# The end of an MoE block: dividing eight expert rows per token between VectorE and TensorE, and moving a gate to GpSimd

## The chip, the cores and the metric

The kernel runs on one core of one Trainium2 chip. The metric is device time in microseconds (us) of one execution, on-chip from start to finish. A core has TensorE (PE, matrix products into PSUM), VectorE (DVE), ScalarE (ACT), GpSimd (POOL) and SyncE (SP), which here only issues DMA transfers. The engines run their own instruction streams and meet at semaphores.

## What is computed

Two transformer layers (feed-forward, attention, per-layer gates) and then a third block that ends in a mixture of experts, all in float32, for 512 tokens of width 1024. The change touches only what comes after the last expert. In the reference:

```
out = jnp.zeros((T + 1, D), jnp.float32).at[rows].add(ys * wts[:, None])   # routed_experts: top 8 of 64 experts
return (routed + shared).reshape(B, S, D).astype(h.dtype)                  # moe_ffn
x = x + g2 * moe_ffn(h, ...)                                               # second_block
return rmsnorm_2(x, final_g)
```

So for each token: shared-expert row, plus eight weighted expert rows, times the gate g2, plus the residual x, and an RMS norm of the sum.

## The kernel before

The kernel is written out by hand per engine. Each engine's order is the order of the Python code, and each semaphore wait is explicit. Up to about 3293 us of 3352 it is bound by TensorE, which runs every product as three (high and low parts). The change begins behind that.

**Layout.** The 512 tokens are four tiles t = 0..3 of 128 tokens (one per partition) by 1024 values. Each expert block's outputs are scattered by GpSimd's indirect DMA to a DRAM tensor `slot_rows`[t, token, slot k, 1024], where slot k = 0..7 is the token's k-th expert in order of expert number. At the end the 32 pieces (t, k), 512 KB each, are fetched back by SyncE in the order of its code, into 16 buffers `rows[0..15]` in `big` and `h_buf`: first the 16 "early" ones, k = 0..3, then 16 "late" ones in the order of the table `LATE`. Late fetch number i waits until buffer i has been read.

**Adding.** `sh_tok[t]` (in `xn_buf`) holds the shared expert's row. VectorE adds slots 0, 1, 3 and 4 into it, one `scalar_tensor_tensor` per tile and slot (`add_row`). TensorE adds slots 2, 5, 6 and 7 in PSUM, as products with a diagonal matrix of the slot's weights (`sum_rows`; `eye_w`, made by ScalarE); one tile and slot is 2 products of 512 columns, which the chip runs as 4 MATMUL instructions. Between its first four pieces and the rest stand 44 small products (`keep_clock`) that do no work.

**Finishing.** `gated_early` (VectorE, two instructions per tile): y = sh_tok * g2, then y + x. `add_late`: the PSUM sum * g2 into `x_tok` (in `mixed_buf`), then y + that. ScalarE squares and sums y and takes the root (`fin["std"]`). `final_norm`: reciprocal, then y * inverse * gain in two halves of 512. SyncE sends each finished tile out. All four early gates stand ahead of the first `add_late`; from there VectorE alternates `add_late(t)` and `final_norm(t - 1)`. GpSimd has nothing to do after its last scatter.

**Semaphores.** `fin["row"]` counts VectorE's adds, `fin["part"]` TensorE's early ones, `fin["mm"]` finished tiles in PSUM, `fin["sum"]` finished sums; `row_in`, `row_last` count landings (16 each); `o_out[s]` tells that a scatter has landed.

Of the kernel before, what the change touches and what calls it, by code (L numbers as in the profile page):

```python
# [129 lines left out]
def block_kernel(nc, dr, out, stop_at=None):  # L130
    with ExitStack() as ctx:
# [320 lines left out]
        fin = {n: sem(f"fin_{n}") for n in ("row", "part", "mm", "sum", "std", "y")}  # L452
# [21 lines left out]
        LATE = [(t, 4) for t in range(TT)] + [(t, k) for t in range(TT) for k in range(5, TOP_K)]  # L474
        PE_ROWS = [2, 5, 6, 7]
# [109 lines left out]
        def _(sp):  # L585
# [59 lines left out]
            for st in STAGES:  # L645
# [50 lines left out]
                elif st == "moe":  # L696
# [73 lines left out]
                    for i, (t, k) in enumerate(LATE):  # L770
                        if i == 0:
                            for s in range(2):
                                after(o_out[s], more * 16 + 16)
# [4 lines left out]
                        if 8 <= i < 12:
                            sp.wait_ge(fin["part"], i - 7)
                        else:  # L780
                            sp.wait_ge(fin["row"], (i if i < 8 else i - 4) + 1)
                        fetch(rows[i], t, k, row_last[t] if k == 4 else row_in[t])
# [816 lines left out]
        def _(act):  # L1599
# [277 lines left out]
            for st in STAGES:  # L1877
# [75 lines left out]
                elif st == "moe":  # L1953
# [112 lines left out]
                    for t in range(TT):  # L2066
                        act.wait_ge(fin["sum"], t + 1)
                        link(nc.scalar.activation(sil_buf[:, :], sh_tok[:, t, :], ACT.Square, accum_out=ssq[:, t:t + 1]))
                        nc.scalar.activation(sdev[:, t:t + 1], ssq[:, t:t + 1], ACT.Sqrt, bias=eps[:, 0:1], scale=1.0 / D
                                             ).then_inc(fin["std"], 1)  # L2070

        @block.gpsimd
        def _(pool):
# [47 lines left out]
            for st in STAGES:  # L2122
# [16 lines left out]
                else:  # L2139
# [64 lines left out]

        @block.vector
        def _(dve):
# [680 lines left out]
            def add_row(n):  # L2888
                k, t = (0, 1, 3, 4)[n // TT], n % TT
                if k == 4:  # L2890
                    dve.wait_ge(row_last[t], 16)
                elif t == 0:
                    dve.wait_ge(row_in[k], 64)
                if n >= TT:
                    dve.wait_ge(fin["row"], n - TT + 1)
                w = slot_w[:, t * TOP_K + k:t * TOP_K + k + 1]
                nc.vector.scalar_tensor_tensor(out=sh_tok[:, t, :], in0=late_row[t, k] if k == 4 else rows[k * TT + t], scalar=w,
                                               in1=sh_tok[:, t, :], op0=ALU.mult, op1=ALU.add).then_inc(fin["row"], 1)

            def combine():  # L2900
                for n in range(EARLY * TT):
                    add_row(n)

                def gated_early(t):
                    y = sh_tok[:, t, :]
                    dve.wait_ge(fin["row"], 3 * TT + t + 1)
                    link(nc.vector.tensor_tensor(y, y, g2_row, ALU.mult))
                    link(nc.vector.tensor_tensor(y, y, x_tok[:, t, :], ALU.add))

                def add_late(t):  # L2910
                    y = sh_tok[:, t, :]
                    dve.wait_ge(fin["mm"], t + 1)
                    link(nc.vector.tensor_tensor(x_tok[:, t, :], ps_t[:, 2 * t * T:2 * t * T + D], g2_row, ALU.mult))
                    nc.vector.tensor_tensor(y, y, x_tok[:, t, :], ALU.add).then_inc(fin["sum"], 1)
# [288 lines left out]
```

## Time and profile before

| what | us |
|---|---|
| median of 3 runs (lowest, highest) | 3352.76 (3351.64, 3355.06) |
| profiled execution, whole | 3353.4 |
| its span, first to last instruction | 3351.6 |
| PE / DVE / ACT / POOL busy | 3266.6 / 1933.7 / 1720.9 / 1341.5 |
| DMA rate in the last four of 40 slices | 389, 372, 367, 300 GB/s |

The table shows a kernel whose TensorE is 97% busy over the whole span. That says nothing of the last 50 us, which have other limits and are read from the timeline of that stretch. In the views, L12 is line 12 of the kernel; "x8" after a row is a run of eight merged instructions; square brackets give the idle time of the engine before the row and what ended it.

### The profile page before, as it was taken

What the parts mean: (1) busy time and instruction counts of PE and PEld (TensorE: products, weight loads), DVE (VectorE), ACT (ScalarE), POOL (GpSimd) and SP (SyncE); (2) the same over time, 40 slices, a digit from 0 to 9 for tenths busy, and PEclk for the clock granted to TensorE, in tenths of its full rate; (3) what the DMA queues carried; (4) which work ended last, traced back from release to release, by engine and by line L of the source; (5) the groups of instructions that cost most, each with busy time, mean ns of one, the idle gap of its engine ahead of it and who ended that gap; (6) DMA issues with size and microseconds to landing.
All of it is one profiled execution on the core that took longest, in us unless ns stands there. A gap on an engine that the chain in (4) does not pass through costs nothing.

```text
span 3351.6 us, 48653 instructions
## 1 busy us (share of the span) xinstructions
PE 3266.6 (97%) x16528; PEld 2637.9 (79%) x16528; DVE 1933.7 (58%) x2446; ACT 1720.9 (51%) x2086; POOL 1341.5 (40%) x675
## 2 busy tenths in 40 slices
PE   8999999999999999999999999999899999999997
PEld 7888887778888788888778888788776788888785
DVE  4335684653354433551473333456676799999898
ACT  5552334555523555321545542512452788888884
POOL 3444442044444444444134444344212344444441
PEclk9999999999999999999999999999999999999999
DMA  3224331022244222443322233223102899999997
GB/s 126 99 95 162 126 104 51 15 93 94 100 155 136 86 95 99 144 144 113 126 76 94 100 94 94 94 88 111 39 20 107 332 377 385 384 391 389 372 367 300
DMA packets 128100, 534.42 MB, mean 159 GB/s; under 512 B 24464, under 2 KB 24720, under 8 KB 100112
## 3 DMA queue, kind: packets, MB, share of 16 engines
q1 hardware_dynamic: 107136, 499.63, 41.8%
q0 software_dynamic: 20736, 33.60, 2.7%
q8 instruction: 52, 0.85, 0.1%
q14 instruction: 32, 0.26, 0.0%
q10 hardware_dynamic: 144, 0.08, 0.0%
HBM read 531.64 MB, written 41.94 MB: 171 GB/s over the span
## 4 chain that ended last, share of the span: by engine, by line
PE 55%; issue 27%; POOL 9%; DVE 4%; DMA 3%; ACT 1%; POOLq 0%; SPq 0%; DVEq 0%; ACTq 0%
PE ps L873 15%; PE ps L875 15%; PE ps L874 15%; POOL w_lo L2085 9%; DMA big<-in_exp_gu 2%; PE ps L1447 2%; PE ps L1045 1%; PE ps L1070 1%; PE ps L1055 1%; PE ps L893 1%; PE ps L1177 1%; PE ps L1215 1%; PE ps L1431 0%; DMA big<-slot_rows 0%; PE ps L1131 0%
## 5 line engine op out<-in xcount | busy, mean ns | idle before, releaser
L2085 POOL TENSOR_TENSOR w_lo<-stage_buf,w_hi 128x1024 fp32r<-128x1024 f32 (+1 forms) x396 | 970.4, 2451 | 1493.0 <-ACT w_hi L1611 1493.0
L1611 ACT ACTIVATE w_hi<-stage_buf 128x1024 fp32r<-128x1024 f32 (+1 forms) x396 | 413.9, 1045 | 1184.5 <-PE ps L875 1122.3
L873 PE MATMUL ps<-x_hi,w_hi 128*128 128x512 f32 x1984 | 774.3, 390 | 4.3 <-POOL w_lo L2085 2.8
L874 PE MATMUL ps<-x_lo,w_hi 128*128 128x512 f32 x1984 | 773.0, 390 | 0.0
L875 PE MATMUL ps<-x_hi,w_lo 128*128 128x512 f32 x1984 | 772.9, 390 | 0.0
L873 PE MATMUL ps<-hid,w_hi 128*128 128x512 f32 x1312 | 519.4, 396 | 2.8 <-issue 1.7
L875 PE MATMUL ps<-hid,w_lo 128*128 128x512 f32 x1312 | 512.2, 390 | 0.0
L874 PE MATMUL ps<-hid,w_hi 128*128 128x512 f32 x1312 | 511.5, 390 | 0.0
L873 PEld LDWEIGHTS ps<-x_hi,w_hi 128*128 128x128 f32 x1984 | 372.6, 188 | 85.2 <-POOL w_lo L2085 3.9
L875 PEld LDWEIGHTS ps<-x_hi,w_lo 128*128 128x128 f32 x1984 | 372.6, 188 | 77.2
L874 PEld LDWEIGHTS ps<-x_lo,w_hi 128*128 128x128 f32 x1984 | 372.7, 188 | 76.7
L2349 DVE TENSOR_TENSOR sq_buf<-ps,rstd 128x512 f32<-128x512 f32 x88 | 60.9, 692 | 406.2 <-PE ps L875 398.9
L873 PEld LDWEIGHTS ps<-hid,w_hi 128*128 128x128 f32 x1312 | 246.5, 188 | 55.0 <-issue 4.6
L875 PEld LDWEIGHTS ps<-hid,w_lo 128*128 128x128 f32 x1312 | 246.4, 188 | 52.7
L874 PEld LDWEIGHTS ps<-hid,w_hi 128*128 128x128 f32 x1312 | 246.9, 188 | 49.0 <-issue 0.2
L2354 DVE TENSOR_TENSOR hid<-tmp_buf,hid 128x512 f32 x88 | 164.3, 1867 | 82.6 <-ACT hid L1702 82.6
L2171 POOL DMA_INDIRECT slot_rows<-stage_buf,mask x72 | 184.6, 2563 | 24.8 <-issue 20.5
L2154 POOL CAST mask<-mask 128x2 int32 (+2 forms) x77 | 71.0, 922 | 308.0 <-PE ps L1447 242.1
L2844 DVE TENSOR_TENSOR hid<-s_buf,hid 128x2048 fp32r<-128x2048 f32 x71 | 162.7, 2292 | 16.1 <-ACT hid L1997 14.8
L2844 DVE TENSOR_TENSOR hid<-big,hid 128x2048 fp32r<-128x2048 f32 x72 | 161.7, 2285 | 9.4 <-ACT hid L1997 9.4
L2844 DVE TENSOR_TENSOR hid<-h_buf,hid 128x2048 fp32r<-128x2048 f32 x72 | 161.6, 2284 | 0.5 <-ACT hid L1997 0.5
L2220 DVE TENSOR_TENSOR acc<-acc,sq_buf 128x512 f32<-128x512 f32 x64 | 152.4, 2381 | 2.2
(401 smaller groups left out, 4858.3 us busy)
## 6 DMA issues: line engine op xcount, KB each, us to landing
stage_buf<-in_gu SPq DMA_DIRECT2D x176, 512.0 KB, 3.2
big<-in_exp_gu SPq DMA_DIRECT2D x72, 1024.0 KB
h_buf<-in_exp_gu SPq DMA_DIRECT2D x72, 1024.0 KB, 12.7
s_buf<-in_exp_dn SPq DMA_DIRECT2D x72, 1024.0 KB
stage_buf<-in_down SPq DMA_DIRECT2D x64, 512.0 KB, 3.6
stage_buf<-in_down SPq DMA_DIRECT2D x32, 384.0 KB, 3.2
sil_buf<-in_ada SPq DMA_DIRECT2D x24, 512.0 KB, 4.0
tmp_buf<-in_ada SPq DMA_DIRECT2D x24, 512.0 KB, 4.2
```

Source lines behind the costliest of these rows:

```text
L873: nc.tensor.matmul(o, a_hi, b_hi, start=start, stop=False)
L874: nc.tensor.matmul(o, a_hi, b_lo, start=False, stop=False)
L875: return nc.tensor.matmul(o, a_lo, b_hi, start=False, stop=stop)
L1447: last = nc.tensor.transpose(ps[:, k // 4, (k % 4) * P:(k % 4) * P + P], xg[s][:, k * P:k * P + P], eye[:, :])
L1611: nc.scalar.activation(w_hi[s][:, 0:n], stage[s][:, 0:n], ACT.Copy).then_inc(upper_done, 1)
L2085: nc.gpsimd.tensor_tensor(w_lo[s][:, 0:n], stage[s][:, 0:n], w_hi[s][:, 0:n].bitcast(F32), ALU.subtract).then_inc(parted, 1)
L2154: nc.gpsimd.tensor_copy(idx[:, s, c0:c1], table[:, b, c0:c1]).then_inc(bk["staged"], 1)
L2171: nc.gpsimd.indirect_dma_start(out=dr["slots"].rearrange("t p k n -> (t p k) n"), out_offset=bass.IndirectOffsetOnAxis(ap=idx[:, at, 1:2], ...
L2220: link(nc.vector.tensor_tensor(acc[:, :], acc[:, :], sq[:, 0, :], ALU.add))
L2349: nc.vector.tensor_tensor(sq[:, 1, :], ps[:, 1, :], rstd[:, :], ALU.mult).then_inc(evac_done, 1)
L2354: nc.vector.tensor_tensor(hid_buf[:, bass.ds(i * T + NF * T, T)], tmp[:, 0, :], hid_buf[:, bass.ds(i * T, T)].bitcast(F32), ALU.subtract). ...
L2844: nc.vector.tensor_tensor(raw_lo[j], raw[s][j], raw_hi[j].bitcast(F32), ALU.subtract).then_inc(raw_parted[j], 1)
```

## The change

- **Division of slots.** VectorE adds slots 0, 2, 4, 6; TensorE slots 1, 3, 5, 7. Each still adds 16 pieces.
- **Order of the late fetches.** `LATE` was (0..3, 4), then (0,5) (0,6) (0,7) (1,5) ... It is now (0,4) (0,6) (0,5) (0,7) (1,4) (1,6) (1,5) (1,7) (2,4) (2,6) (3,4) (3,6) (2,5) (2,7) (3,5) (3,7): pairs for VectorE and for TensorE in turn. The engines wait for a pair at a time; the last piece, (3,7), has a wait of its own. Fetch (3,4) waits in addition for VectorE's first late add, because its landing semaphore is used a second time.
- **Gate and residual** (y * g2, + x) move from VectorE to GpSimd, two instructions per tile, as soon as VectorE has added that tile's two late slots. The values are the same.
- **VectorE's order** is now: early adds, late pairs of tiles 0, 1, 2, `add_late(0)`, late pair of tile 3, `add_late(1)`, `final_norm(0)`, and so on; the last tile's `add_late` is done in halves of 512, and so are ScalarE's squares of it.
- **TensorE** has no `keep_clock` products any more.

```diff
-        PE_ROWS = [2, 5, 6, 7]
...
+        DVE_ROWS, PE_ROWS = [0, 2, 4, 6], [1, 3, 5, 7]
+        dve_landed = [(row_last[0], 32), (row_last[2], 32), (row_in[0], 96), (row_last[0], 64)]
+        pe_landed = [(row_last[1], 32), (row_last[3], 32), (row_in[1], 96), (row_in[3], 80)]
+        final_landed = (row_in[2], 80)
...
-                        if 8 <= i < 12:
-                            sp.wait_ge(fin["part"], i - 7)
-                        else:
-                            sp.wait_ge(fin["row"], (i if i < 8 else i - 4) + 1)
-                        fetch(rows[i], t, k, row_last[t] if k == 4 else row_in[t])
+                        slot, at = i // TT, i % TT
+                        sp.wait_ge(fin["part" if slot in PE_ROWS else "row"], slot // 2 * TT + at + 1)
+                        if (t, k) == (TT - 1, 4):
+                            sp.wait_ge(fin["row"], 2 * TT + 1)
+                        final = (t, k) == (TT - 1, TOP_K - 1)
+                        fetch(rows[i], t, k, (final_landed if final else pe_landed[t] if k in PE_ROWS else dve_landed[t])[0])
...
-                pe.wait_ge(row_in[2], 64)
-                for t in range(TT):
-                    add(t, 0, rows[2 * TT + t]).then_inc(fin["part"], 1)
-                keep_clock(0, 44, add=True)
-                for t in range(TT):
-                    pe.wait_ge(row_in[t], 64 + 48)
-                    for j in range(1, 4):
-                        last = add(t, j, late_row[t, PE_ROWS[j]])
-                    last.then_inc(fin["mm"], 1)
+                for j, k in enumerate(PE_ROWS[:2]):
+                    pe.wait_ge(row_in[k], 64)
+                    for t in range(TT):
+                        add(t, j, rows[k * TT + t]).then_inc(fin["part"], 1)
+                for t in range(TT - 1):
+                    pe.wait_ge(*pe_landed[t])
+                    add(t, 2, late_row[t, PE_ROWS[2]])
+                    add(t, 3, late_row[t, PE_ROWS[3]]).then_inc(fin["mm"], 1)
+                t = TT - 1
+                pe.wait_ge(*pe_landed[t])
+                add(t, 2, late_row[t, PE_ROWS[2]])
+                pe.wait_ge(*final_landed)
+                for c in range(2):
+                    add(t, 3, late_row[t, PE_ROWS[3]], (c,)).then_inc(fin["mm"], 1)
...
+                    t = TT - 1
+                    act.wait_ge(fin["sum"], TT)
+                    link(nc.scalar.activation(sil_buf[:, 0:T], sh_tok[:, t, 0:T], ACT.Square, accum_out=half_ssq))
+                    link(nc.scalar.activation(half_mean, half_ssq, ACT.Identity, bias=eps[:, 0:1], scale=1.0 / D))
+                    act.wait_ge(fin["sum"], TT + 1)
+                    link(nc.scalar.activation(sil_buf[:, T:D], sh_tok[:, t, T:D], ACT.Square, accum_out=ssq[:, t:t + 1]))
+                    nc.scalar.activation(sdev[:, t:t + 1], ssq[:, t:t + 1], ACT.Sqrt, bias=half_mean, scale=1.0 / D
+                                         ).then_inc(fin["std"], 1)
...
+                    for t in range(TT):
+                        y = sh_tok[:, t, :]
+                        pool.wait_ge(fin["row"], 2 * TT + 2 * t + 2)
+                        link(nc.gpsimd.tensor_tensor(y, y, g2_row, ALU.mult))
+                        nc.gpsimd.tensor_tensor(y, y, x_tok[:, t, :], ALU.add).then_inc(fin["gated"], 1)
...
+                def late_rows(t):
+                    dve.wait_ge(*dve_landed[t])
+                    for j, k in enumerate(DVE_ROWS[2:]):
+                        dve.wait_ge(fin["row"], 2 * TT + 2 * t + 1 if j else TT + t + 1)
+                        add_row(t, k, late_row[t, k])
+                def add_late(t, a=0, n=D):
+                    y, x = sh_tok[:, t, a:a + n], x_tok[:, t, a:a + n]
+                    dve.wait_ge(fin["gated"], t + 1)
+                    dve.wait_ge(fin["mm"], t + 1 + a // T)
+                    link(nc.vector.tensor_tensor(x, ps_t[:, 2 * t * T + a:2 * t * T + a + n], g2_row[:, a:a + n], ALU.mult))
+                    nc.vector.tensor_tensor(y, y, x, ALU.add).then_inc(fin["sum"], 1)
...
-                for t in range(TT):
-                    gated_early(t)
-                for t in range(TT):
-                    add_late(t)
-                    if t >= 1:
-                        final_norm(t - 1)
-                final_norm(TT - 1)
+                for t in range(3):
+                    late_rows(t)
+                add_late(0)
+                late_rows(3)
+                add_late(1)
+                final_norm(0)
+                add_late(2)
+                final_norm(1)
+                for c in range(2):
+                    add_late(3, c * T, T)
+                final_norm(2)
+                final_norm(3)
```

VectorE's stream behind the early adds. Names: `xn_buf` is sh_tok, `rot` holds g2, `mixed_buf` is x_tok, `ps` is PSUM; a row without "big" or "h_buf" is gate, residual or norm. Before:

```order
L2897 SCALAR_TENSOR_TENSOR xn_buf<-big,pt_buf,xn_buf 128x1024 [waits fin_row,row_in3]
L2897 SCALAR_TENSOR_TENSOR xn_buf<-big,pt_buf,xn_buf 128x1024 [waits fin_row] x3
L2897 SCALAR_TENSOR_TENSOR xn_buf<-big,pt_buf,xn_buf 128x1024 [waits fin_row,row_last0]
L2897 SCALAR_TENSOR_TENSOR xn_buf<-big,pt_buf,xn_buf 128x1024 [waits fin_row,row_last1]
L2897 SCALAR_TENSOR_TENSOR xn_buf<-big,pt_buf,xn_buf 128x1024 [waits fin_row,row_last2]
L2897 SCALAR_TENSOR_TENSOR xn_buf<-big,pt_buf,xn_buf 128x1024 [waits fin_row,row_last3]
L2907 TENSOR_TENSOR xn_buf<-xn_buf,rot 128x1024 [waits fin_row]
L2908 TENSOR_TENSOR xn_buf<-xn_buf,mixed_buf 128x1024 [waits dve_own]
L2907 TENSOR_TENSOR xn_buf<-xn_buf,rot 128x1024 [waits fin_row,dve_own]
L2908 TENSOR_TENSOR xn_buf<-xn_buf,mixed_buf 128x1024 [waits dve_own]
L2907 TENSOR_TENSOR xn_buf<-xn_buf,rot 128x1024 [waits fin_row,dve_own]
L2908 TENSOR_TENSOR xn_buf<-xn_buf,mixed_buf 128x1024 [waits dve_own]
L2907 TENSOR_TENSOR xn_buf<-xn_buf,rot 128x1024 [waits fin_row,dve_own]
L2908 TENSOR_TENSOR xn_buf<-xn_buf,mixed_buf 128x1024 [waits dve_own]
L2913 TENSOR_TENSOR mixed_buf<-ps,rot 128x1024 [waits fin_mm,dve_own]
L2914 TENSOR_TENSOR xn_buf<-xn_buf,mixed_buf 128x1024 [waits dve_own]
```

After (L2915 is `add_row`, L2936 and L2937 are `add_late`):

```order
L2915 SCALAR_TENSOR_TENSOR xn_buf<-big,pt_buf,xn_buf 128x1024 [waits fin_row] x3
L2915 SCALAR_TENSOR_TENSOR xn_buf<-big,pt_buf,xn_buf 128x1024 [waits fin_row,row_last0]
L2915 SCALAR_TENSOR_TENSOR xn_buf<-big,pt_buf,xn_buf 128x1024 [waits fin_row]
L2915 SCALAR_TENSOR_TENSOR xn_buf<-h_buf,pt_buf,xn_buf 128x1024 [waits fin_row,row_last2]
L2915 SCALAR_TENSOR_TENSOR xn_buf<-h_buf,pt_buf,xn_buf 128x1024 [waits fin_row]
L2915 SCALAR_TENSOR_TENSOR xn_buf<-big,pt_buf,xn_buf 128x1024 [waits fin_row,row_in0]
L2915 SCALAR_TENSOR_TENSOR xn_buf<-big,pt_buf,xn_buf 128x1024 [waits fin_row]
L2936 TENSOR_TENSOR mixed_buf<-ps,rot 128x1024 [waits fin_mm,fin_gated]
L2937 TENSOR_TENSOR xn_buf<-xn_buf,mixed_buf 128x1024 [waits dve_own]
L2915 SCALAR_TENSOR_TENSOR xn_buf<-big,pt_buf,xn_buf 128x1024 [waits fin_row,row_last0]
L2915 SCALAR_TENSOR_TENSOR xn_buf<-big,pt_buf,xn_buf 128x1024 [waits fin_row]
L2936 TENSOR_TENSOR mixed_buf<-ps,rot 128x1024 [waits fin_mm,fin_gated]
L2937 TENSOR_TENSOR xn_buf<-xn_buf,mixed_buf 128x1024 [waits dve_own]
```

The eight rows on `rot` and `mixed_buf` between the adds and the first `ps` row are gone, and each pair of late adds waits for one landing semaphore. `add_late` now also waits for GpSimd (`fin_gated`).

GpSimd's last rows, after its last scatter (L2190, the same instruction as L2171 before). Before, the stream ended with that scatter. After:

```order
L2174 REGISTER_ALU
L2190 DMA slot_rows<-stage_buf,mask 4096x1024 [waits bk_staged]
L2226 TENSOR_TENSOR xn_buf<-xn_buf,rot 128x1024 [waits fin_row]
L2227 TENSOR_TENSOR xn_buf<-xn_buf,mixed_buf 128x1024 [waits pool_own]
L2226 TENSOR_TENSOR xn_buf<-xn_buf,rot 128x1024 [waits fin_row]
L2227 TENSOR_TENSOR xn_buf<-xn_buf,mixed_buf 128x1024 [waits pool_own]
```

Eight instructions stand here now, two per tile (the first two tiles are shown); all read two operands in SBUF (`xn_buf` with `rot`, `xn_buf` with `mixed_buf`).

SyncE's late fetches, from the first on. Before:

```order
L753 DMA big<-slot_rows 128x1024 [waits o_out0,o_out1,fin_row]
L753 DMA big<-slot_rows 128x1024 [waits fin_row] x3
L753 DMA h_buf<-slot_rows 128x1024 [waits fin_row]
L756 REGISTER_ALU
L753 DMA h_buf<-slot_rows 128x1024 [waits o_out0,fin_row]
L753 DMA h_buf<-slot_rows 128x1024 [waits o_out1,fin_row]
L753 DMA h_buf<-slot_rows 128x1024 [waits fin_row]
L753 DMA big<-slot_rows 128x1024 [waits fin_part] x4
L753 DMA big<-slot_rows 128x1024 [waits fin_row] x4
```

After:

```order
L758 DMA big<-slot_rows 128x1024 [waits o_out0,o_out1,fin_row]
L761 REGISTER_ALU
L758 DMA big<-slot_rows 128x1024 [waits o_out0,fin_row]
L758 DMA big<-slot_rows 128x1024 [waits fin_row]
L758 DMA big<-slot_rows 128x1024 [waits o_out1,fin_row]
L758 DMA h_buf<-slot_rows 128x1024 [waits fin_part] x4
L758 DMA big<-slot_rows 128x1024 [waits fin_row] x4
L758 DMA big<-slot_rows 128x1024 [waits fin_part] x4
```

The waits for the last two scatters (`o_out0`, `o_out1`) moved from the sixth and seventh late fetch to the second and fourth. The four fetches into `h_buf` and the last four now wait for TensorE (`fin_part`).

## Rows read from the trace of the kernel before

**Rows 1.** Timeline, VectorE, last 50 us: start, length, instruction, count, idle before.
```profile
3312.49 9.66 DVE L2897 SCALAR_TENSOR_TENSOR xn_buf<-big,pt_buf,xn_buf 128x1024 f32<-128x1024 f32 x8 [4.98 <-DMA big<-slot_rows]
3322.07 1.22 DVE L2907 TENSOR_TENSOR xn_buf<-xn_buf,rot 128x1024 f32<-128x1024 f32 x1
...
3330.88 1.23 DVE L2908 TENSOR_TENSOR xn_buf<-xn_buf,mixed_buf 128x1024 f32<-128x1024 f32 x1
3332.14 1.22 DVE L2913 TENSOR_TENSOR mixed_buf<-ps,rot 128x1024 f32<-128x1024 f32 x1
...
3338.97 1.22 DVE L2913 TENSOR_TENSOR mixed_buf<-ps,rot 128x1024 f32<-128x1024 f32 x1
...
3342.89 1.22 DVE L2913 TENSOR_TENSOR mixed_buf<-ps,rot 128x1024 f32<-128x1024 f32 x1
...
3347.77 0.75 DVE L2921 SCALAR_TENSOR_TENSOR mixed_buf<-xn_buf,small,rstd 128x512 f32<-128x512 f32 x1
```
**Rows 2.** Groups by line, VectorE, 3312 to 3352 us: busy us, mean ns, idle before.
```profile
L2897 DVE SCALAR_TENSOR_TENSOR xn_buf<-big,pt_buf,xn_buf 128x1024 f32<-128x1024 f32 x8 | 9.7, 1280 | 5.0 <-DMA big<-slot_rows 5.0
...
L2907 DVE TENSOR_TENSOR xn_buf<-xn_buf,rot 128x1024 f32<-128x1024 f32 x4 | 4.9, 1224 | 0.1
L2913 DVE TENSOR_TENSOR mixed_buf<-ps,rot 128x1024 f32<-128x1024 f32 x4 | 4.9, 1219 | 0.0
```
**Rows 3.** Timeline, SyncE, 3293 to 3352 us.
```profile
3339.08 9.80 SPq L786 DMA_DIRECT2D out<-mixed_buf  x4
```
**Rows 4.** Source line of the fetches, windows of one: start, then us to landing.
```profile
L753 SPq DMA_DIRECT2D big<-slot_rows x1: 320/320/320, 3300.4 to 3300.4; - x1
...
DMA to landing us min/median/max: 14.7/14.7/14.7
...
L753 SPq DMA_DIRECT2D h_buf<-slot_rows x1: 320/320/320, 3308.0 to 3308.0; - x1
...
L753 SPq DMA_DIRECT2D h_buf<-slot_rows x1: 320/320/320, 3310.3 to 3310.3; - x1
...
L753 SPq DMA_DIRECT2D big<-slot_rows x1: 429/429/429, 3319.2 to 3319.2; - x1
...
DMA to landing us min/median/max: 13.9/13.9/13.9
```
**Rows 5.** Timeline, TensorE, 3300 to 3345 us.
```profile
3307.39 6.39 PE L1512 MATMUL ps<-big,tmp_buf 128*128 128x512 f32 x8 [6.35 <-DMA big<-slot_rows]
...
3321.85 7.03 PE L1512 MATMUL ps<-h_buf,tmp_buf 128*128 128x512 f32 x16
...
3332.15 10.46 PE L1512 MATMUL ps<-big,sq_buf 128*128 128x512 f32 x24
```
**Rows 6.** Windows: length, busy of PE, PEld, DVE, ACT, POOL, clock, DMA.
```profile
3302.00:3306.00 4.00, 0.00 (x0) 0.00 (x0) 4.00 (x4) 0.09 (x1) 1.56 (x2) 1.00 0.99 354
3306.00:3312.00 6.00, 4.61 (x6) 2.06 (x7) 1.51 (x2) 0.00 (x0) 0.00 (x0) 0.50 1.03 417
```
**Rows 7.** GpSimd's two-operand instructions: timeline at 2187 us, group, one source line.
```profile
2187.36 4.71 POOL L2085 TENSOR_TENSOR w_lo<-stage_buf,w_hi 128x1024 fp32r<-128x1024 f32 x2 [20.73 <-ACT w_hi L1611]
...
L2085 POOL TENSOR_TENSOR w_lo<-stage_buf,w_hi 128x1024 fp32r<-128x1024 f32 x364 | 906.8, 2492 | 1412.9 <-ACT w_hi L1611 1412.8
...
L2098 POOL TENSOR_TENSOR pt_buf<-pt_buf,sil_buf x2: 627/628/629, 2374.2 to 2375.5; 128x256 f32<-128x256 f32 x2
```
**Rows 8.** Timeline around 290 us, VectorE and GpSimd; last, durations (min/median/max) of L2220.
```profile
290.41 0.69 DVE L2219 TENSOR_TENSOR sq_buf<-h_buf 128x512 f32 x1
291.14 2.77 DVE L2220 TENSOR_TENSOR acc<-acc,sq_buf 128x512 f32<-128x512 f32 x1
...
290.58 2.78 POOL L2085 TENSOR_TENSOR w_lo<-stage_buf,w_hi 128x1024 fp32r<-128x1024 f32 x1 [1.69 <-ACT w_hi L1611]
...
L2220 DVE TENSOR_TENSOR acc<-acc,sq_buf x64: 691/2766/2866, 275.9 to 2533.9; 128x512 f32<-128x512 f32 x64
```
**Rows 9.** Timeline, VectorE, 2187.0 to 2192.5 us, beside the first row of 7.
```profile
2188.04 0.69 DVE L2394 TENSOR_SCALAR big<-ps 128x512 f32<-128x512 f32 x1 [1.12 <-PE ps L893]
```

More of the change, by code:

```diff
@@ L451, in block_kernel @@
         row_last = [sem(f"row_last{t}") for t in range(TT)]
-        fin = {n: sem(f"fin_{n}") for n in ("row", "part", "mm", "sum", "std", "y")}
+        fin = {n: sem(f"fin_{n}") for n in ("row", "part", "gated", "mm", "sum", "std", "y")}
         RAW = 2048
@@ L473, in block_kernel @@
         last_hi, last_lo = raw_hi[0], raw_lo[0]
-        LATE = [(t, 4) for t in range(TT)] + [(t, k) for t in range(TT) for k in range(5, TOP_K)]
-        PE_ROWS = [2, 5, 6, 7]
+        LATE = [(t, k) for t in range(2) for k in (4, 6, 5, 7)] + [(t, k) for t in (2, 3) for k in (4, 6)] + [
+            (t, k) for t in (2, 3) for k in (5, 7)]
+        DVE_ROWS, PE_ROWS = [0, 2, 4, 6], [1, 3, 5, 7]
+        dve_landed = [(row_last[0], 32), (row_last[2], 32), (row_in[0], 96), (row_last[0], 64)]
+        pe_landed = [(row_last[1], 32), (row_last[3], 32), (row_in[1], 96), (row_in[3], 80)]
+        final_landed = (row_in[2], 80)
         late_row = {tk: rows[i] for i, tk in enumerate(LATE)}
@@ L482, in block_kernel @@
         ssq, sdev, sinv = small[:, 64:68], small[:, 68:72], small[:, 72:76]
+        half_ssq, half_mean = small[:, 76:77], small[:, 77:78]
         before, iota_t = mask[:, 0:P], mask[:, P:P + T]
@@ L1508, in sum_rows, with add @@
             def sum_rows():
-                def add(t, j, row):
-                    for c in range(2):
+                def add(t, j, row, cs=(0, 1)):
+                    for c in cs:
                         done = nc.tensor.matmul(ps[:, 2 * t + c, :], eye_w[4 * t + j], row[:, c * T:(c + 1) * T],
@@ L2065, in _ @@
                     evacuate(1, more_n + 1)
-                    for t in range(TT):
+                    for t in range(TT - 1):
                         act.wait_ge(fin["sum"], t + 1)
@@ L2886, in routed @@
                 hidden_low(1, more_n + 1)
[L2888 to L2892, printed above, removed]
-                    dve.wait_ge(row_in[k], 64)
[L2894 to L2914, printed above, removed]
+            def add_row(t, k, row):
+                w = slot_w[:, t * TOP_K + k:t * TOP_K + k + 1]
+                nc.vector.scalar_tensor_tensor(out=sh_tok[:, t, :], in0=row, scalar=w, in1=sh_tok[:, t, :],
+                                               op0=ALU.mult, op1=ALU.add).then_inc(fin["row"], 1)
@@ new lines, in combine @@
+            def combine():
+                for j, k in enumerate(DVE_ROWS[:2]):
+                    dve.wait_ge(row_in[k], 64)
+                    for t in range(TT):
+                        if j:
+                            dve.wait_ge(fin["row"], t + 1)
+                        add_row(t, k, rows[k * TT + t])
+                def late_rows(t):
[9 more added lines that the diff above has]
+                    nc.vector.tensor_tensor(y, y, x, ALU.add).then_inc(fin["sum"], 1)
@@ L2923, in final_norm @@
                     ins.then_inc(fin["y"], 1)
-                for t in range(TT):
-                    gated_early(t)
-                for t in range(TT):
-                    add_late(t)
-                    if t >= 1:
-                        final_norm(t - 1)
-                final_norm(TT - 1)
+                for t in range(3):
[10 more added lines that the diff above has]
+                final_norm(3)
             for st in STAGES:
```

## The prediction

> **What bounds the kernel now.** I read the timeline of the last 50 us first, engine by engine, because the whole-span shares (TensorE 97%) describe what lies ahead of the change. VectorE's rows [rows 1] are the ones to see: from 3312.49, when the pieces it had waited 4.98 us for land, to 3348.52 (3347.77 + 0.75) it runs without a gap worth naming. In those 36.0 us stand 8 adds (9.66), 8 instructions of gate and residual (3322.07 to 3332.14, 10.1) and the late sums and norms (16.4). Every other engine only has to stay ahead of it. The groups by line [rows 2] give the prices: 1.28 us for an add as recorded, 1.22 for a 1024-wide two-operand instruction; back to back an add takes 9.66 / 8 = 1.21. SyncE's last rows [rows 3] are four output transfers, and the span ends 3.1 us behind VectorE's last instruction (3351.6 - 3348.5). Two things lie close behind: the landings of the fetches [rows 4], the last issued at 3319.2 and landed 13.9 later, at 3333.1; and TensorE, which works until 3342.6 (3332.15 + 10.46) [rows 5], 0.3 us before VectorE takes up its last tile at 3342.89 [rows 1].
>
> **The landings.** The late piece fetched at 3300.4 lands at 3315.1, the last at 3333.1: 14 pieces later in 18.0 us, 1.29 us each, with the transfer engines full (share 0.99 and 1.03) [rows 4, 6]. The change moves the same bytes, so I keep this raster of landings and only put other pieces on it. The new order needs its second late fetch at the moment a scatter has landed, which before was the fetch at 3308.0, and its fourth at 3310.3 [rows 4]. At 3308.0 the early slot 3 and (0,4) are still under way, to 3313.8, so the queue is not empty and (0,6) lands at 3315.1. From there (1,4) and (1,6) are down by 3320, (2,4) and (2,6) by 3325, (3,4) and (3,6) by 3327.6, the last by 3333.1. The extra wait of (3,4) for VectorE's first late add ends near 3316.3, with eight pieces (10 us) still queued: it costs nothing. The fetches behind TensorE's slot 3 can be issued from 3314 to 3320, also in time.
>
> **TensorE.** It starts on slot 1 near 3302.2 rather than on slot 2 at 3307.39, and drops the 44 idle products. A 512-wide instruction is 7.03 / 16 = 0.44 us at the full clock, 6.39 / 8 = 0.80 where the granted clock was 0.50 [rows 5, 6]; that low clock followed 5 us in which TensorE did nothing (1.00 still in 3302 to 3306) [rows 6]. A piece is 4 instructions, 1.8 us. Slot 1: to 3309.3; wait for slot 3's landing at 3312.5; slot 3: to 3319.6; tile 0: 3323.3; tile 1: 3326.9; tile 2 lands at 3330.2 and is done at 3333.8; the last tile is done at 3337.5. The idle spells are now 3.2 and 3.3 us, shorter than the one of 5 that lowered the clock. I cost the dropped products at nothing: VectorE, below, asks for tile 0 at 3331 and for the last at 3351. If that cover goes, half clock from the start is 64 x 0.80 = 51 us, to 3353.4.
>
> **VectorE's own work after the change.** By 3312.2 it has added slots 0 and 2 (slot 2 lands at 3307.4, where TensorE's wait for it ended [rows 5], and four adds take 4.8), so it stands where it stood before. Then: 8 late adds at 1.2, four of them behind their own predecessor (+0.07), 9.9; four late sums, three of 2.45 and the last in halves, 2.8, makes 10.1; four norms, 6.2, from the raster 3338.97 to 3342.89 = 3.92 for one sum and one norm [rows 1]. Sum 26.2. Removed: 10.1 of gate and residual. ScalarE's squares of the last half hide behind `final_norm(2)`, as before.
>
> **What the move to GpSimd costs.** The price of one instruction is in the trace: a GpSimd subtraction of two 1024-wide SBUF operands takes 4.71 / 2 = 2.36 us back to back, and a multiplication of 256 columns in place 0.63, the same rate [rows 7]. Eight of them are 18.8 us, which would fit beside VectorE if the two ran side by side. They don't. At 290.58 [rows 8] GpSimd starts while a VectorE instruction with SBUF operands runs until 291.10; it needs 2.78 instead of 2.36 and ends at 293.36, 2.26 behind VectorE's end. VectorE's next one, L2220, which also takes both operands from SBUF, starts at 291.14 and ends at 293.91, 0.55 behind GpSimd: 2.77 us for 0.69 of work. That is no accident of one place: the median of its 64 instances is 2.766, the least 0.691 [rows 8]. A VectorE instruction that reads PSUM, at 2188.04 in the middle of a GpSimd one, keeps its 0.69 [rows 7, 9]. So two-SBUF-operand instructions of the two engines exclude each other, whole instruction by whole instruction. All late adds, the second half of each late sum and both halves of each norm are of that kind; only the products with `ps` are not.
>
> The Trainium skill says the same of the cause (SBUF — State Buffer, "Who interferes with whom"): a VectorE instruction with two SBUF inputs and a GpSimd instruction that reads SBUF share a read port as an exclusive lock, and the later one is blocked fully. [...] The skill also warns (Perfetto Trace Analysis, "GPSIMD Engine Instruction") that GpSimd's recorded durations are unreliable and that spacing should be used; by the recorded mean of 2.49 instead of the spacing of 2.36, eight would be 1.0 us more.
>
> **The schedule.** At 3315.1 VectorE adds tile 0's pair, to 3317.5. GpSimd's first instruction (3317.6 to 3320.0) falls into VectorE's wait for tile 1 (2.4 us, free of charge). Then they alternate. VectorE stands behind GpSimd: 2.3 us before its second add of tile 1; 1.9 and 2.3 around tile 2's pair; 1.2 in `add_late(0)` (the `ps` product covers the rest); 2.3 before tile 3's pair; 1.2 in `add_late(1)`; 2.1 in `final_norm(0)`. Sum 13.3, from 3321 to 3345.4, when GpSimd is through. Each blocked one ends 0.14 sooner after its release than it takes alone (0.55 against 0.69 [rows 8]), seven times, -0.9. Landing waits are 2.4 and 0.5.
>
> 3315.1 + 26.2 + 13.3 - 0.9 + 2.9 = 3356.6, against 3348.5: +8.1 us. In terms: 10.1 saved; 13.3 - 0.9 lost to exclusion; 5.5 of waiting for landings where VectorE had work before (3312.5 to 3315.1, and 2.9); 0.6 for the halves and the pairs' own order; minus 0.4 that VectorE waited for the root of tile 0. The span becomes 3359.7 and the execution 3361.5, as the profiled one was 3353.4 for a span of 3351.6. That one lies 0.6 above the median of 3352.76, so the forecast is 3360.8.
>
> **Rivals.**
> - *Exclusion does not bite here (the other side: not slower).* If GpSimd's instructions ran freely, the schedule has no blocked time and waits 2.4 and 2.7 for landings: 3315.1 + 26.2 + 5.1 = 3346.4, -2.1: 3350.6. It decides from 5 us of blocked time downward. For it: the last 50 us themselves show no exclusion, since GpSimd computes nothing there. Against: the median of L2220's 64 instances. 0.08.
> - *VectorE wins the turns and GpSimd fills the gaps.* Then the bound is the sum of excluding work from 3315.1: GpSimd 8 x 2.26 = 18.1, VectorE 8 x 1.2 + 4 x 1.15 + 8 x 0.67 = 19.6, plus little of the last `ps` halves: 3353.5, +5.0: 3357.8. For it: GpSimd, too, is the one that waits in rows 8. Against: there it got the very next turn. 0.16.
> - *The fetches run dry.* SyncE issues in order; the two scatter waits now stand ahead of 14 fetches rather than 10. If a scatter lands 5 us later, VectorE's pairs shift by 3 to 5 us: 3364 to 3366. Against: the fetches still under way at 3308.0. 0.08.
> - *TensorE stays at the low clock* without its filler: 3353.4 for its end, then the last half sum, root and norm, 4.2: 3357.6, beyond the schedule by 1.0: 3361.8. 0.04.
>
> **How the numbers follow.** The schedule above has 0.64, its own range is 3358.5 to 3363.5. A measurement of this kernel can tell 0.2%, 6.7 us, from no change. Of the 0.64 I put 0.56 beyond that and 0.08 within; the freed-port rival gives 0.06 within and 0.02 faster; the second 0.15 within, 0.01 slower; the last two 0.12 slower. Faster 0.02, same 0.29, slower 0.69. The range 3355 to 3366 leaves out the first rival and little else.
>
> **What would show it.** Right: L2915's late adds, L2937 and L2944 with durations of 2 to 3.5 us where GpSimd's L2226 and L2227 run, L2936 at 1.2 throughout; GpSimd done near 3345; VectorE's last instruction near 3356.6; TensorE idle and no one waiting for it. Wrong: L2937 and the late adds at 1.2 with GpSimd's beside them (then the kernel is slightly faster); VectorE waiting for landings past 3326 (then the fetch order is the matter); VectorE waiting for `ps` (then the clock is).

## The result, and the profile after

The changed kernel is slower: 3362.66 us, median of 9 runs (3358.29 to 3369.93), against 3354.28 us (3351.15 to 3355.26) of before beside it. The ratio is 1.0026, 95% interval 1.0017 to 1.0034. The forecast was 3360.8. The profiled execution took 3360.6 us, its span (first to last instruction) is 3358.8.

Executions differ by several us before the changed part begins (VectorE's first slot-0 add started at 3297.87 before and 3297.51 after, and between 3293.69 and 3301.92 in the kernels below). So all traces are compared by the **tail**: from the start of that first add to the end of VectorE's last instruction. Before it is 50.65 us (3297.87, in the row below, to 3348.52 [rows 1]); after it is 58.2 (3297.51 to 3355.71), so +7.5. Behind VectorE's last instruction the span has 3.1 us more in both. The row of before, of VectorE's timeline:

```profile
3297.87 4.86 DVE L2897 SCALAR_TENSOR_TENSOR xn_buf<-big,pt_buf,xn_buf 128x1024 f32<-128x1024 f32 x4
```

VectorE's timeline after (start, length, instruction, count, idle before); it answers to [rows 1]:

```profile
3297.51 4.86 DVE L2915 SCALAR_TENSOR_TENSOR xn_buf<-big,pt_buf,xn_buf 128x1024 f32<-128x1024 f32 x4
3306.67 4.87 DVE L2915 SCALAR_TENSOR_TENSOR xn_buf<-big,pt_buf,xn_buf 128x1024 f32<-128x1024 f32 x4 [4.29 <-DMA big<-slot_rows]
3314.40 2.60 DVE L2915 SCALAR_TENSOR_TENSOR xn_buf<-big,pt_buf,xn_buf 128x1024 f32<-128x1024 f32 x2 [2.86 <-DMA big<-slot_rows]
3319.52 4.74 DVE L2915 SCALAR_TENSOR_TENSOR xn_buf<-h_buf,pt_buf,xn_buf 128x1024 f32<-128x1024 f32 x2 [2.52 <-DMA h_buf<-slot_rows]
3324.61 6.43 DVE L2915 SCALAR_TENSOR_TENSOR xn_buf<-big,pt_buf,xn_buf 128x1024 f32<-128x1024 f32 x2 [0.36 <-DMA big<-slot_rows]
3330.96 1.21 DVE L2936 TENSOR_TENSOR mixed_buf<-ps,rot 128x1024 f32<-128x1024 f32 x1
3332.21 2.34 DVE L2937 TENSOR_TENSOR xn_buf<-xn_buf,mixed_buf 128x1024 f32<-128x1024 f32 x1
3334.47 4.70 DVE L2915 SCALAR_TENSOR_TENSOR xn_buf<-big,pt_buf,xn_buf 128x1024 f32<-128x1024 f32 x2
3339.09 1.22 DVE L2936 TENSOR_TENSOR mixed_buf<-ps,rot 128x1024 f32<-128x1024 f32 x1
3340.34 2.33 DVE L2937 TENSOR_TENSOR xn_buf<-xn_buf,mixed_buf 128x1024 f32<-128x1024 f32 x1
...
3342.78 2.65 DVE L2944 SCALAR_TENSOR_TENSOR mixed_buf<-xn_buf,small,std 128x512 f32<-128x512 f32 x1
3345.35 0.74 DVE L2944 SCALAR_TENSOR_TENSOR mixed_buf<-xn_buf,small,rstd 128x512 f32<-128x512 f32 x1
3346.01 1.21 DVE L2936 TENSOR_TENSOR mixed_buf<-ps,rot 128x1024 f32<-128x1024 f32 x1
3347.26 1.22 DVE L2937 TENSOR_TENSOR xn_buf<-xn_buf,mixed_buf 128x1024 f32<-128x1024 f32 x1
...
3354.96 0.75 DVE L2944 SCALAR_TENSOR_TENSOR mixed_buf<-xn_buf,small,rstd 128x512 f32<-128x512 f32 x1
```

GpSimd's gate and residual in the same timeline. Before, this stretch had no such rows; the nearest were [rows 7]:

```profile
3317.09 2.34 POOL L2226 TENSOR_TENSOR xn_buf<-xn_buf,rot 128x1024 f32<-128x1024 f32 x1 [12.84 <-DVE xn_buf L2915]
3319.51 2.34 POOL L2227 TENSOR_TENSOR xn_buf<-xn_buf,mixed_buf 128x1024 f32<-128x1024 f32 x1
3324.33 2.35 POOL L2226 TENSOR_TENSOR xn_buf<-xn_buf,rot 128x1024 f32<-128x1024 f32 x1 [2.48 <-DVE xn_buf L2915]
3326.76 3.20 POOL L2227 TENSOR_TENSOR xn_buf<-xn_buf,mixed_buf 128x1024 f32<-128x1024 f32 x1
3331.12 2.35 POOL L2226 TENSOR_TENSOR xn_buf<-xn_buf,rot 128x1024 f32<-128x1024 f32 x1 [1.16 <-DVE xn_buf L2915]
3333.54 3.22 POOL L2227 TENSOR_TENSOR xn_buf<-xn_buf,mixed_buf 128x1024 f32<-128x1024 f32 x1
3339.25 2.34 POOL L2226 TENSOR_TENSOR xn_buf<-xn_buf,rot 128x1024 f32<-128x1024 f32 x1 [2.48 <-DVE xn_buf L2915]
3341.67 3.21 POOL L2227 TENSOR_TENSOR xn_buf<-xn_buf,mixed_buf 128x1024 f32<-128x1024 f32 x1
```

Read the two together. Wherever a VectorE row with two SBUF operands begins inside a GpSimd row, it is long, and it ends about 1.1 us (1024 columns) or 0.55 us (512) behind GpSimd's end: L2937 from 3332.21 to 3334.55, GpSimd to 3333.47; L2944 from 3342.78 to 3345.43, GpSimd to 3344.88. L2936, which reads PSUM, keeps its 1.21 and 1.22 although GpSimd starts 0.16 us behind it, and GpSimd keeps its 2.35 and 2.34. With GpSimd through at 3344.88, a sum (3347.26) takes 1.22 and a norm half (3345.35) 0.74. Taken one by one, the pairs "4.74", "6.43" and "4.70" hold four long adds (the first of the pair in the first and the last, both in the middle one: 3.42, 3.15, 3.25, 3.38 us, against 1.28). With two late sums (2.34, 2.33 against 1.22) and one norm half (2.65 against 0.75) that makes seven blocked instructions, with this much time beyond what they take alone: 2.14 + 1.87 + 1.97 + 2.10 + 1.12 + 1.11 + 1.90 = 12.2 us.

TensorE's timeline after, to [rows 5], and two windows with the granted clock (the third number from the right), to [rows 6]. The timeline:

```profile
3301.80 3.70 PE L1518 MATMUL ps<-h_buf,tmp_buf 128*128 128x512 f32 x8 [1.11 <-ACT stage_buf L2042]
3305.34 3.60 PE L1518 MATMUL ps<-h_buf,sq_buf 128*128 128x512 f32 x8
3311.87 5.40 PE L1518 MATMUL ps<-big,tmp_buf 128*128 128x512 f32 x8 [2.93 <-DMA big<-slot_rows]
3317.10 3.60 PE L1518 MATMUL ps<-big,sq_buf 128*128 128x512 f32 x8
...
3329.75 8.83 PE L1518 MATMUL ps<-big,sq_buf 128*128 128x512 f32 x16 [2.18 <-DMA big<-slot_rows]
```

The windows:

```profile
3313.00:3317.00 4.00, 4.00 (x6) 1.56 (x6) 2.57 (x2) 0.00 (x0) 0.00 (x0) 0.58 1.03 410
3329.00:3334.00 5.00, 4.25 (x6) 1.82 (x7) 4.96 (x3) 0.00 (x0) 3.76 (x3) 0.66 0.40 161
```

Eight instructions took 5.40 us instead of 3.70: the granted clock fell to the half level (1.2 of 2.4 GHz) behind each of the two idle spells, 2.93 and 2.18 us. Taken by single us it was 0.50 from 3313 to 3316 and from 3331 to 3333, and 1.00 in both spells themselves. TensorE is done at 3338.58 all the same, 11 us before VectorE asks for the last tile (3349.92).

### The profile page after: what moved, and what is told of

Read it like the earlier page. It is cut to its first block, busy times and chain, and to the rows that moved or that the text cites. A ratio compares the mean times of both kernels' runs of the same rounds, so it can differ in the third digit from the quotient of the medians.

```text
span 3358.8 us, 48572 instructions
## 1 busy us (share of the span) xinstructions
PE 3265.3 (97%) x16484; PEld 2635.6 (78%) x16484; DVE 1934.2 (58%) x2440; ACT 1721.0 (51%) x2089; POOL 1361.2 (41%) x683
## 4 chain that ended last, share of the span: by engine, by line
issue 48%; PE 32%; POOL 15%; DVE 3%; DMA 1%; ACT 1%; POOLq 1%; SPq 0%; DVEq 0%; ACTq 0%
POOL w_lo L2104 15%; PE ps L879 8%; PE ps L881 8%; PE ps L880 8%; PE ps L1453 2%; DMA big<-slot_rows 1%; PE ps L1221 1%; PE ps L1183 1%; PE ps L1137 0%; PE ps L1472 0%; PE ps L1327 0%; PE ps L1437 0%; PE ps L1145 0%; POOLq L581 0%; DVE xn_buf L2915 0%
## 5 line engine op out<-in xcount | busy, mean ns | idle before, releaser
L2190 POOL DMA_INDIRECT slot_rows<-stage_buf,mask x72 | 184.7, 2565 | 24.9 <-issue 20.6
```

What stands on the lines that cost most here:

```text
L2190: nc.gpsimd.indirect_dma_start(out=dr["slots"].rearrange("t p k n -> (t p k) n"), out_offset=bass.IndirectOffsetOnAxis(ap=idx[:, at, 1:2], ...
```

## The experiments

Theory: the +7.5 is VectorE's removed work (-10.1) against exclusion by GpSimd (+12.2), more waiting (10.0 us for landings, against 5.0 for landings and 0.4 for a root before: +4.6) and the halves and the pairs' own order (+0.8). All kernels below are measured by the tail of one trace each, beside the timed ratio. Where a ratio's interval includes 1, as in the first three, the whole time shows no difference from before, and what is said of gains and losses against before rests on the tail; all three intervals lie below the changed kernel's (1.0017 to 1.0034).

**Gate and residual back on VectorE, the rest as changed.**

```diff
-                    for t in range(TT):
-                        y = sh_tok[:, t, :]
-                        pool.wait_ge(fin["row"], 2 * TT + 2 * t + 2)
-                        link(nc.gpsimd.tensor_tensor(y, y, g2_row, ALU.mult))
-                        nc.gpsimd.tensor_tensor(y, y, x_tok[:, t, :], ALU.add).then_inc(fin["gated"], 1)
...
+                    y = sh_tok[:, t, :]
+                    dve.wait_ge(fin["row"], 2 * TT + 2 * t + 2)
+                    link(nc.vector.tensor_tensor(y, y, g2_row, ALU.mult))
+                    nc.vector.tensor_tensor(y, y, x_tok[:, t, :], ALU.add).then_inc(fin["gated"], 1)
```

> The changed kernel with gate and residual back on VectorE, behind each tile's late pair; everything else of the change stays. Theory (instructions of GpSimd and VectorE with two SBUF operands exclude each other): no VectorE instruction lasts longer than 1.3 us, the 10.1 us of gate work fills the landing waits of 2.5 us each, VectorE ends near 3351 instead of 3355.7; time about 3356, 5 us under the changed kernel and 2 to 3 over before. Rival (the new fetch order and the waits by pairs are what costs, GpSimd's share is hidden): the time stays at 3360 or rises to 3365, as VectorE gets 10 us more work.

Measured: 3354.32 us, ratio to before 1.0006 (0.9996 to 1.0016); tail 53.4, +2.7. The tail is as expected (2 to 3 over before); the time is 1.7 under the 3356 that was expected. VectorE's timeline:

```profile
3303.05 4.87 DVE L2910 SCALAR_TENSOR_TENSOR xn_buf<-big,pt_buf,xn_buf 128x1024 f32<-128x1024 f32 x4 [4.50 <-DMA big<-slot_rows]
...
3315.90 2.61 DVE L2910 SCALAR_TENSOR_TENSOR xn_buf<-h_buf,pt_buf,xn_buf 128x1024 f32<-128x1024 f32 x2
3318.55 1.22 DVE L2928 TENSOR_TENSOR xn_buf<-xn_buf,rot 128x1024 f32<-128x1024 f32 x1
...
3327.28 1.23 DVE L2936 TENSOR_TENSOR xn_buf<-xn_buf,mixed_buf 128x1024 f32<-128x1024 f32 x1
```

No instruction is long any more. VectorE waits for landings 4.50 and then 2.87 before the first late pair, 7.4 in all, against 4.98 for landings and 0.43 for a root before: +2.0. The other 0.8 is left for the pairs' own order and the halves. With the gate's work on VectorE the two later waits of the changed kernel (2.52 and 0.36) are filled. So 4.8 of the 7.5 come with the move to GpSimd, and 2.7 with the new division and order.

**Only the move to GpSimd, the rest as before.**

```diff
+                    for t in range(TT):
+                        y = sh_tok[:, t, :]
+                        pool.wait_ge(fin["row"], 3 * TT + t + 1)
+                        link(nc.gpsimd.tensor_tensor(y, y, g2_row, ALU.mult))
+                        nc.gpsimd.tensor_tensor(y, y, x_tok[:, t, :], ALU.add).then_inc(fin["gated"], 1)
...
+                    dve.wait_ge(fin["gated"], t + 1)
...
-                for t in range(TT):
-                    gated_early(t)
```

The added wait stands in `add_late`.

> The kernel before with one part of the change alone: gate and residual on GpSimd, each tile after its fourth add by VectorE; late sums wait for them. Theory: GpSimd's eight instructions start at 3318.5 and take turns with VectorE until about 3344; VectorE's last adds, late sums and the first norm last 2 to 3.5 us; VectorE ends near 3352 instead of 3348.5, time 3356 to 3357, although VectorE has 10 us less work. Rival (no exclusion): VectorE waits for TensorE's last tile at 3342.6 and ends where it did, 3348.5; no change.

Measured: 3355.82 us, ratio 1.0007 (0.9999 to 1.0016); tail 53.1, +2.5. VectorE's rows:

```profile
3316.43 13.84 DVE L2902 SCALAR_TENSOR_TENSOR xn_buf<-big,pt_buf,xn_buf 128x1024 f32<-128x1024 f32 x8 [4.87 <-DMA big<-slot_rows]
3331.01 1.23 DVE L2913 TENSOR_TENSOR mixed_buf<-ps,rot 128x1024 f32<-128x1024 f32 x1 [0.74 <-PE ps L1512]
...
3336.16 1.23 DVE L2913 TENSOR_TENSOR mixed_buf<-ps,rot 128x1024 f32<-128x1024 f32 x1 [2.59 <-PE ps L1512]
...
3339.28 2.65 DVE L2921 SCALAR_TENSOR_TENSOR mixed_buf<-xn_buf,small,std 128x512 f32<-128x512 f32 x1
3341.86 2.83 DVE L2921 SCALAR_TENSOR_TENSOR mixed_buf<-xn_buf,small,rstd 128x512 f32<-128x512 f32 x1
3344.61 1.21 DVE L2913 TENSOR_TENSOR mixed_buf<-ps,rot 128x1024 f32<-128x1024 f32 x1
3345.86 2.13 DVE L2914 TENSOR_TENSOR xn_buf<-xn_buf,mixed_buf 128x1024 f32<-128x1024 f32 x1
```

GpSimd's rows:

```profile
3322.59 3.32 POOL L2207 TENSOR_TENSOR xn_buf<-xn_buf,rot 128x1024 f32<-128x1024 f32 x1 [13.76 <-DVE xn_buf L2902]
...
3341.35 2.79 POOL L2207 TENSOR_TENSOR xn_buf<-xn_buf,rot 128x1024 f32<-128x1024 f32 x1
3344.22 2.68 POOL L2208 TENSOR_TENSOR xn_buf<-xn_buf,mixed_buf 128x1024 f32<-128x1024 f32 x1
```

The eight adds take 13.84 instead of 9.66, both halves of a norm are blocked (2.65 and 2.83 against 0.75), and three late sums (1.30, 1.75 and 2.13) lose 1.5: 9.7 us blocked. The product with `ps` at 3344.61 starts in the middle of a GpSimd instruction and keeps its 1.21. VectorE, with its own work gone, also comes 3.3 too early for TensorE's tiles. Less the 10.1 that left it, less 0.5 of waits of before (the root and 0.1 of the landing): +2.4. So by the tail the move gains nothing even by itself, in the order it had: it costs 2.5. The two parts alone make 5.2 and together 7.5. In the new order the move blocks 2.5 us more (12.2 against 9.7) and opens 2.9 of landing waits that the gate fills when it is on VectorE; against that, the 2.8 of waits that the move adds in the old order (3.3 less 0.5) are not there. The three make 2.6, against the 2.3 measured.

**GpSimd busy about as long, but only writing.** Gate and residual are left out of the computation; two memsets per tile stand in their place, under the same waits, with one more wait for the tile before.

```diff
-    link(nc.gpsimd.tensor_tensor(y, y, g2_row, ALU.mult))
-    nc.gpsimd.tensor_tensor(y, y, x_tok[:, t, :], ALU.add).then_inc(fin["gated"], 1)
+    if t:
+        pool.wait_ge(fin["gated"], t)
+    link(nc.gpsimd.memset(big[:, 0:2560], 0.0))
+    nc.gpsimd.memset(big[:, 0:2560], 0.0).then_inc(fin["gated"], 1)
```

Measured: 3351.18 us, ratio 0.9996 (0.9986 to 1.0005); tail 48.2, -2.5. GpSimd's timeline:

```profile
3329.87 2.23 POOL L2229 MEMSET big<- 128x2560 f32 x1
3332.49 2.23 POOL L2228 MEMSET big<- 128x2560 f32 x1 [0.39 <-DVE xn_buf L2917]
```

VectorE's:

```profile
3324.92 2.60 DVE L2917 SCALAR_TENSOR_TENSOR xn_buf<-big,pt_buf,xn_buf 128x1024 f32<-128x1024 f32 x2 [2.51 <-DMA big<-slot_rows]
...
3329.84 2.60 DVE L2917 SCALAR_TENSOR_TENSOR xn_buf<-big,pt_buf,xn_buf 128x1024 f32<-128x1024 f32 x2
...
3333.60 1.22 DVE L2939 TENSOR_TENSOR xn_buf<-xn_buf,mixed_buf 128x1024 f32<-128x1024 f32 x1
```

The pair at 3329.84 and the sum at 3333.60 run beside a memset and keep 2.60 and 1.22. So it is neither that GpSimd is busy nor its semaphores. What VectorE waited for is an instruction that reads SBUF. The memset differs in one more thing, it writes `big` and not `xn_buf`; but in [rows 8] the two engines touched different buffers and VectorE was blocked all the same, so it is the reading and not the common buffer. Against the changed kernel the tail is 10.0 shorter; that is the 12.2 of blocked time less 2.1 of landing waits that VectorE now meets (2.51 and 2.51, instead of 2.52 and 0.36). The -2.5 is also about what the whole change would have been worth had GpSimd's instructions blocked nothing.

**TensorE's clock held up.** The changed kernel with 24 idle products again between TensorE's slots 1 and 3.

```diff
+                    if j == 0:
+                        keep_clock(0, 24, add=True)
```

> Only change against the changed kernel: 24 of the small idle products of TensorE (2.78 us in the kernel with five slots on TensorE) stand again between its slots 1 and 3, so that TensorE's first idle spell of 2.9 us goes. My theory (TensorE is off the path, its half clock behind that spell cost nothing): the pieces of slot 3 stand 1.8 us apart instead of some 2.7 at first, TensorE's granted clock is 1.00 until at least 3322, and VectorE's rows stay as they are: from its first slot-0 add to its last instruction 58.2 us, as in the changed kernel (57.8 to 58.6), the kernel's time as the changed one's. Rival (the low clock of TensorE delays the fetches behind slot 3 or the last tiles and carries a part of the slowdown): that stretch shrinks by 1 us or more, to 57.2 or less.

Measured: 3359.82 us, ratio 1.0015 (1.0006 to 1.0024); tail 58.3 (3298.34 to 3356.63). TensorE:

```profile
3309.62 2.78 PE L821 MATMUL ps<-zeros 128*128 128x256 bf16 x24
3312.81 3.70 PE L1518 MATMUL ps<-big,tmp_buf 128*128 128x512 f32 x8 [0.41 <-DMA big<-slot_rows]
...
3331.46 9.74 PE L1518 MATMUL ps<-big,sq_buf 128*128 128x512 f32 x16 [4.65 <-DMA big<-slot_rows]
```

Slot 3 ran at the full clock (3.70 instead of 5.40) and VectorE's tail did not move by more than 0.1. TensorE only reached its second wait earlier, waited 4.65 instead of 2.18, and took its last tiles at the half clock for longer (granted 0.50 from 3331 to 3336). The low clock is off the path.

**The changed kernel once more, beside it.** The same program.

> The changed kernel itself, timed beside the others. The stretch from VectorE's first slot-0 add to its last instruction was 58.2 us, 7.5 more than before; the whole kernel was measured 1.0026 of before. If the part that was changed is all that differs, this one is slower than before by 7.5 of 3354, a ratio of 1.0022, and the stretch is 58.2 again (57.9 to 58.5). Rival (part of the difference is scatter of what lies ahead of the change): a ratio below 1.0015 or above 1.0030 with the same stretch.

Measured: 3362.28 us, ratio 1.0022 (1.0013 to 1.0031); tail 58.4 (3299.55 to 3357.95). The tail comes back within 0.2, and the ratio is what 7.5 to 7.7 us of 3354 give. Its interval overlaps that of the kernel with the clock held (1.0015), so the two ratios tell nothing of the clock; the tails do.

**Five slots on TensorE, three on VectorE, gate and residual on VectorE.** Built from the changed kernel: slots 0, 2, 4 on VectorE, 1, 3, 5, 6, 7 on TensorE, the fetches in an order to match, gate and residual back on VectorE behind each tile's late add, the last tile in halves, 24 idle products. The order of the late fetches and the division:

```diff
-        LATE = [(t, k) for t in range(2) for k in (4, 6, 5, 7)] + [(t, k) for t in (2, 3) for k in (4, 6)] + [
-            (t, k) for t in (2, 3) for k in (5, 7)]
-        DVE_ROWS, PE_ROWS = [0, 2, 4, 6], [1, 3, 5, 7]
...
+        LATE = [(0, 4), (0, 5), (0, 6), (1, 4), (0, 7), (1, 5), (2, 4), (1, 6), (1, 7), (3, 4), (2, 5), (2, 6), (2, 7), (3, 5),
+                (3, 6), (3, 7)]
+        DVE_ROWS, PE_ROWS = [0, 2, 4], [1, 3, 5, 6, 7]
```

> A version made from what the above points to: GpSimd does nothing, VectorE does gate and residual in its landing waits, TensorE adds five slots (1, 3, 5, 6, 7) and VectorE three (0, 2, 4), 24 idle products between TensorE's slots 1 and 3 keep its clock, last tile in halves. Theory: TensorE ends near 3341, VectorE near 3345 to 3347; time 3350 to 3351, 2 to 4 us under before. Rival (TensorE at the low clock after idle spells of 3 us, as in the changed kernel): TensorE ends 3344, time 3353 to 3354.

Measured: 3350.74 us, ratio 0.9989 (0.9980 to 0.9997); tail 47.54, -3.1. It beats both kernels, if by little. TensorE's last rows:

```profile
3329.81 7.25 PE L1513 MATMUL ps<-big,sq_buf 128*128 128x512 f32 x16
3336.89 5.31 PE L1513 MATMUL ps<-big,pt_buf 128*128 128x512 f32 x12
```

VectorE's, the longest wait left among the late adds and the end:

```profile
3315.51 1.28 DVE L2905 SCALAR_TENSOR_TENSOR xn_buf<-big,pt_buf,xn_buf 128x1024 f32<-128x1024 f32 x1 [1.61 <-DMA big<-slot_rows]
...
3346.52 0.74 DVE L2937 SCALAR_TENSOR_TENSOR mixed_buf<-xn_buf,small,rstd 128x512 f32<-128x512 f32 x1
```

Four adds of 1.2 leave VectorE (-4.8) for TensorE, which has time; 1.1 of waits and about 0.6 for halves and order come back. TensorE, at full speed, is done at 3342.2, and VectorE takes up the last half sum at 3342.81: the two now end nearly together, so a sixth slot would hardly fit. No run tried it.

## Why the prediction was right

- **The whole time.** The forecast is 1.0024 of the 3352.76 that it started from; measured was 1.0026. The medians are 8.4 us apart and the tails 7.5; the interval of the ratio (1.0017 to 1.0034) covers both.
- **The landings.** The first late pair was forecast for 3315.1, the last piece for 3333.1. Counted from the first slot-0 add, as before, VectorE's first late pair begins at 3314.76 (16.89 behind the first add), and the last piece lands 34.7 behind it, before 35.2. The spacing of the landings held; the first was forecast 0.3 too late, the last 0.5.
- **VectorE's own work.** Forecast 26.2 from the first late pair on. From 3314.40 to 3355.71 are 41.3 us; less 12.2 blocked and 2.9 of waits (2.52 + 0.36, forecast 2.4 + 0.5) leaves 26.2.
- **The exclusion.** Forecast 13.3 - 0.9 = 12.4, in seven instructions (seven times 0.14 is 1.0, so the working should say 12.3); measured 12.2, in seven, and VectorE next in turn each time. The places are those named but for one: of tile 1's pair the first add was blocked, not the second. GpSimd was done at 3344.88, forecast 3345.4. The rate from [rows 7] (2.36; here two unblocked ones take 4.76, 2.38 each) and the finish behind GpSimd from [rows 8] (0.55 us for 512 columns) carried over. By the Trainium skill (SBUF — State Buffer, "Who interferes with whom") the cause is a read port held as an exclusive lock. The runs agree with what it says of two instructions that are free of it: a VectorE `tensor_tensor` with one operand in PSUM keeps 1.21 (3344.61, with only the move), and a GpSimd instruction that only writes blocks nothing. The port itself no trace shows.
- **GpSimd's recorded durations.** The Trainium skill (Perfetto Trace Analysis, "GPSIMD Engine Instruction") distrusts them and would go by the spacing of their starts. Here an unblocked one is recorded with 2.34, and the next starts 2.42 behind its start, so for these the two agree; a record of 3.20 has the waiting for VectorE in it.
- **The end.** VectorE's last instruction ended at 3355.71, forecast 3356.6; by the tail +7.5, forecast +8.1. Of the 0.6, 0.3 are landing and 0.2 exclusion.
- **What failed: TensorE's clock.** "The idle spells are now 3.2 and 3.3 us, shorter than the one of 5 that lowered the clock" compared with one instance, and misread it: 5 us is how long TensorE had been idle while the granted clock was still 1.00 [rows 6]; that whole spell was 6.35 [rows 5]. Here spells of 2.93 and 2.18 were followed by the half clock. The last tile was done at 3338.58 rather than 3337.5. The error cost the forecast nothing, because VectorE asked for that tile 11 us later; the run with the clock held up shows the same.

The rivals. *No exclusion* (3350.6) is refuted by the long rows; the memset kernel shows what it would have looked like (3351.18). *VectorE wins the turns* (3357.8) did not happen: GpSimd got its turn whenever it asked, at the latest at the end of VectorE's instruction. *The fetches run dry*: VectorE's last wait for a landing ended at 3324.61. *TensorE stays low*: its clock fell for two stretches, and VectorE never waited for its tiles.

## What to carry to other kernels

Before work is moved from VectorE to GpSimd, look in the trace for a place where both run on SBUF operands: if instructions there stretch to the other engine's length, each moved one can cost VectorE up to 2.1 us where it saves 1.2, so that here VectorE lost 12.2 us for 10.1 saved, although GpSimd had been idle. Add the waits that the work would have filled where it stood. One slot more on TensorE, which had time, did pay. To judge a change of the last 60 us of 3350, compare the stretch from a common instruction in the traces (it repeated within 0.2 us in two traces of the changed kernel) beside the whole time, which in 35 runs of the kernel before spread over 15.

## What was not expected of the hardware

- **The length of an idle spell did not settle TensorE's clock.** The wait ahead of slot 3, and the granted clock behind it: 2.93 us (changed kernel) half; 3.14 (the same kernel again) half; 2.95 (memset kernel) full, eight instructions in 3.70. At the second wait: 2.18 half, 2.24 (again) full. Windows of the memset kernel (first row) and of the second trace of the changed kernel:

```profile
3312.00:3316.00 4.00, 3.84 (x9) 1.82 (x10) 1.28 (x1) 0.00 (x0) 0.00 (x0) 1.00 1.03 411
3314.00:3318.00 4.00, 3.90 (x5) 1.70 (x6) 1.33 (x2) 0.00 (x0) 0.00 (x0) 0.57 1.03 411
3332.00:3336.00 4.00, 3.99 (x10) 1.84 (x11) 3.96 (x3) 0.00 (x0) 2.76 (x3) 1.00 0.25 99
```

  What decides it remains open.
- **GpSimd is given a turn between two instructions of VectorE that stand back to back.** With only the move, 8 queued adds of VectorE let GpSimd in from 3322.59 on, one by one, and GpSimd's first four instructions are 3.2 to 3.3 long (0.9 to 1.0 of waiting). The second norm half, 2.83, was blocked by the GpSimd instruction at 3341.35 although nothing stood between it and the first.
- **A blocked instruction has part of its own time behind the release.** A 1024-wide one ends 1.08 us after GpSimd's end and takes 1.22 alone; a 512-wide one 0.55 and 0.75.
